# Two transformer blocks on one core: one Strassen pair turned into two plain units, tiles placed in another order, and the loading of x rearranged

## The chip, the core and the metric

The kernel runs on one core of a Trainium2 chip. The metric is device time in microseconds of one execution. Before the change the median of three runs is 2495.06 us (2494.91 to 2496.38).

## The reference, cut to what matters

Two blocks over 1024 tokens with 1024 channels, in float32. Block one is gated linear attention beside a short convolution, then a gated feed-forward network of width 2816. Block two is spatial gating beside windowed attention.

```
h = rmsnorm(x, norm1_g); proj = h @ w_in            # 1024 x (2*256 + 2*512 + 16 + 3*512)
gate_logits = p_a @ w_gate_up + b_gate              # p_a: the 16 columns "COL_A = GATE_RANK"
log_a = log_sigmoid(gate_logits) / 16 ; o = gla_chunked(q, k, v, log_a) ...
x = x + concat([o_gla, o_conv]) @ w_out
h2 = rmsnorm(x, norm2_g)
x = x + (silu(h2 @ w_ffn_gate) * (h2 @ w_ffn_up)) @ w_ffn_down
x = rmsnorm(x, norm_f_g)                            # then block two, the same size again
```

## The kernel before

Everything is kept transposed: channels on the 128 partitions, the 1024 tokens along the row. A *unit* is 128 output channels of one projection: 8 slices of the contraction by 2 halves of 512 tokens. Each operand is split into a rounded part and a rest (`x_hi`, `x_lo`, `w_hi`, `w_lo`), and three products are summed, so that a unit is 48 matmuls of 512 columns (L683 hi by hi, L684, L685) into one half, the *slot*, of the PSUM tile `dense` (two slots of two banks). 197 units run in a fixed order. For each, SyncE loads the weights into `w_raw` (`load`), ScalarE makes `w_hi` (`split`, L1028), GpSimd makes `w_lo` (L584), and VectorE takes the result out of PSUM (`scaled`, L1528). Every engine has its own queue in program order, and semaphores join them: `evac` counts results taken out, `mm_done` finished units, `w_lo` split weights.

The gate and up projections of the feed-forward network are 22 tiles of two units each. The first `DIRECT`/2 tiles are plain units. For the others the two units are computed as one *duo*: one level of a Strassen-Winograd scheme over 2x2 quarters, with 7 products of 12 matmuls instead of 8 (84 instead of 96). The products read sums of quarters of x (`x_sums_split`, three of the seven) or quarters of x itself, and the weights' sums are made on VectorE (`weight_sums`, L1716 to L1723). `times` (L831 to L833) issues one product into one of the PSUM banks B7, B5, B1, B6. `hi_half` (ScalarE, L1180) and `lo_half` (GpSimd, L619) fill one of four half-slots of `w_hi` and `w_lo` for one product; `half(p, i)` says which. Product 5 of a duo adds onto bank B7 and waits for `joined`, that is for VectorE's L1773. The raw weights of the duos alternate between `w_raw` and a second buffer in tiles 12 and 13 of `work`.

The finished tiles m go to DRAM (`store_m`) and are read back behind the duos into tiles 12 and 13 of `work` (`load_m`), split (`m_hi` on ScalarE, L1210, `m_lo` on VectorE, L1728), and feed the down projection, whose first unit is U_DOWN.

At the start SyncE asks for the vectors, the weights of unit 0 (the 16 gate columns padded with zeros to 128), x in eight slices with the weights of unit 1 after the fourth, and so on. Unit 0 takes the slices of x as they come; unit 1 follows it. ScalarE writes x_hi (L1059), VectorE x_lo (L1487), then both make the sums of squares for the norm (L1042, L1499), and the token sums (L705) and the spread of the norm's factor (L713) are put between matmuls of units.

Tiles are placed by `place` one behind the other in each partition: x_hi, x_lo (32 KiB each), w_raw, w_hi, w_lo (8 KiB each), then the small tiles vectors (316 bytes), identity, ones, rstd and others, and behind them residual (32 KiB) and work (80 KiB). Worked out from the sizes, work starts 129,856 bytes behind x_hi, which is 31 x 4096 + 2880. x_sums_split, work_split, m_hi, m_lo and the softmax tiles lie inside work; att_q_split, att_k_hi, att_k_lo and att_v_split inside residual.

## Time and profile before

| | us |
|---|---|
| median of three runs | 2495.06 |
| the profiled execution | 2494.21 |
| its span, first to last instruction | 2492.5 |
| TensorE (PE) busy | 2416.4 (97%) |
| PE weight loads (beside the matmuls) | 1987.4 (80%) |
| VectorE (DVE) busy | 1239.6 (50%) |
| ScalarE (ACT) busy | 804.3 (32%) |
| GpSimd (POOL) busy | 644.1 (26%) |
| mean granted TensorE clock, as a share of full speed | 0.987 |

The page's chain of the work that ended last lies on PE for 93% of the span and on DVE for 4%. A matmul's record is longer than the distance to the next one, since they are pipelined: what counts is the distance from start to start. In the rows below a bracket at the end of a line gives the engine's idle time before it and what ended that.

### The profile page before, as it was taken

What the parts mean: (1) busy time and instruction counts of PE and PEld (TensorE: products, weight loads), DVE (VectorE), ACT (ScalarE), POOL (GpSimd) and SP (SyncE); (2) the same over time, 40 slices, a digit from 0 to 9 for tenths busy, and PEclk for the clock granted to TensorE, in tenths of its full rate; (3) what the DMA queues carried; (4) which work ended last, traced back from release to release, by engine and by line L of the source; (5) the groups of instructions that cost most, each with busy time, mean ns of one, the idle gap of its engine ahead of it and who ended that gap; (6) DMA issues with size and microseconds to landing.
All of it is one profiled execution on the core that took longest, in us unless ns stands there. A gap on an engine that the chain in (4) does not pass through costs nothing.

```text
span 2492.5 us, 29802 instructions
## 1 busy us (share of the span) xinstructions
PE 2416.4 (97%) x11248; PEld 1987.4 (80%) x11248; DVE 1239.6 (50%) x1655; ACT 804.3 (32%) x1173; POOL 644.1 (26%) x332
## 2 busy tenths in 40 slices
PE   8999999899999989999999999999999999999997
PEld 6888788678888878888888888877877877878886
DVE  4444673844444443344321102477777787753534
ACT  4422132333233321134211101255555555541221
POOL 2221122345555522222221122111121121122221
PEclk9999899999999999999999999999999999999998
DMA  3111222132222242212222224332322323344223
GB/s 129 43 43 34 85 79 90 66 138 85 92 78 76 77 152 102 85 60 85 101 93 76 78 99 140 100 98 94 118 91 86 110 84 100 110 152 143 92 95 109
DMA packets 66148, 234.63 MB, mean 94 GB/s; under 512 B 7936, under 2 KB 8080, under 8 KB 66064
## 3 DMA queue, kind: packets, MB, share of 16 engines
q1 hardware_dynamic: 51376, 179.98, 22.1%
q10 hardware_dynamic: 14688, 53.48, 5.3%
q8 instruction: 59, 0.97, 0.2%
q14 instruction: 25, 0.20, 0.0%
HBM read 175.76 MB, written 57.67 MB: 94 GB/s over the span
## 4 chain that ended last, share of the span: by engine, by line
PE 93%; DVE 4%; issue 1%; DMA 1%; ACT 1%; DVEq 0%; SPq 0%; POOL 0%; ACTq 0%
PE dense L683 22%; PE dense L685 22%; PE dense L684 22%; PE dense L831 5%; PE dense L833 5%; PE dense L832 5%; PE aux L956 2%; PE aux L940 2%; PE aux L941 1%; PE aux L969 1%; PE aux L968 1%; PE aux L903 1%; DVE residual L1733 1%; DVE att_p_lo L1924 1%; PE aux L713 0%
## 5 line engine op out<-in xcount | busy, mean ns | idle before, releaser
L683 PE MATMUL dense<-x_hi,w_hi 128*128 128x512 f32 x2000 | 809.4, 405 | 14.2 <-DVE x_lo L1487 13.0
L685 PE MATMUL dense<-x_hi,w_lo 128*128 128x512 f32 x2000 | 783.5, 392 | 0.0
L684 PE MATMUL dense<-x_lo,w_hi 128*128 128x512 f32 x2000 | 782.4, 391 | 0.0
L584 POOL TENSOR_TENSOR w_lo<-w_raw,w_hi 128x1024 fp32r<-128x1024 f32 x157 | 382.5, 2436 | 1414.0 <-ACT w_hi L1028 1405.9
L1028 ACT CAST w_hi<-w_raw 128x1024 fp32r<-128x1024 f32 x156 | 163.9, 1051 | 886.2 <-PE dense L685 863.2
L683 PEld LDWEIGHTS dense<-x_hi,w_hi 128*128 128x128 f32 x2000 | 378.1, 189 | 84.9 <-issue 15.3
L685 PEld LDWEIGHTS dense<-x_hi,w_lo 128*128 128x128 f32 x2000 | 377.0, 188 | 81.5
L684 PEld LDWEIGHTS dense<-x_lo,w_hi 128*128 128x128 f32 x2000 | 378.5, 189 | 67.6 <-issue 1.2
L1528 DVE TENSOR_TENSOR work<-dense,rstd 128x1024 f32<-128x1024 f32 x95 | 116.0, 1221 | 401.1 <-PE dense L685 395.2
L619 POOL TENSOR_TENSOR w_lo<-w_sums,w_hi 128x512 fp32r<-128x512 f32 x80 | 122.2, 1539 | 142.8 <-ACT w_hi L1180 142.8
L683 PE MATMUL dense<-work_split,w_hi 128*128 128x512 f32 x352 | 138.0, 392 | 1.1 <-DVE work L1785 1.1
L1356 ACT CAST att_p_hi<-aux 128x512 fp32r<-128x512 f32 x192 | 92.1, 479 | 144.6 <-PE aux L956 144.2
L685 PE MATMUL dense<-work_split,w_lo 128*128 128x512 f32 x352 | 138.2, 393 | 0.0
L831 PE MATMUL dense<-x_hi,w_hi 128*128 128x512 f32 x320 | 128.3, 401 | 9.7 <-DVE work L1773 9.7
L684 PE MATMUL dense<-work_split,w_hi 128*128 128x512 f32 x352 | 137.1, 390 | 0.0
L1924 DVE TENSOR_TENSOR att_p_lo<-aux,att_p_hi 128x512 fp32r<-128x512 f32 x192 | 106.3, 554 | 59.6 <-ACT att_p_hi L1356 57.3
L833 PE MATMUL dense<-x_hi,w_lo 128*128 128x512 f32 x320 | 127.2, 397 | 0.0
L832 PE MATMUL dense<-x_lo,w_hi 128*128 128x512 f32 x320 | 126.8, 396 | 0.0
L1680 DVE TENSOR_TENSOR residual<-dense,residual 128x1024 f32<-128x1024 f32 x32 | 39.2, 1225 | 158.7 <-PE dense L685 158.7
L831 PE MATMUL dense<-x_sums_split,w_hi 128*128 128x512 f32 x240 | 95.9, 400 | 9.7 <-DVE work L1528 9.7
L1346 ACT ACTIVATE att_p_late<-att_p_late,softmax_stats 128x640 f32<-128x640 f32 (+1 forms) x64 | 63.5, 993 | 102.0 <-DVE softmax_stats L1905 101.9
L833 PE MATMUL dense<-x_sums_split,w_lo 128*128 128x512 f32 x240 | 95.1, 396 | 0.0
(236 smaller groups left out, 3318.1 us busy)
## 6 DMA issues: line engine op xcount, KB each, us to landing
w_raw<-weights SPq DMA_DIRECT2D x177, 512.0 KB, 3.8
kept_qkv<-work ACTq DMA_DIRECT2D x24, 512.0 KB, 2.6
kept_m<-work ACTq DMA_DIRECT2D x22, 512.0 KB, 2.6
work<-kept_m SPq DMA_DIRECT2D x22, 512.0 KB, 3.5
w_raw_b<-weights SPq DMA_DIRECT2D x20, 512.0 KB, 4.3
residual<-xT SPq DMA_DIRECT2D x16, 512.0 KB, 6.6
kept_x<-residual ACTq DMA_DIRECT2D x16, 512.0 KB, 2.7
att_q<-kept_qkv SPq DMA_DIRECT2D x32, 256.0 KB, 4.0
```

The costliest lines, as they stand in the source:

```text
L584: pool.tensor_tensor(WL[:, u.slot], WR[:, u.slot], WH[:, u.slot].bitcast(f32), ALU.subtract).then_inc(w_lo, 1)
L619: pool.tensor_tensor(WL[:, h // 2, at4], quarter(p, i), WH[:, h // 2, at4].bitcast(f32), ALU.subtract).then_inc(*((d_lo, 1) if i < 6 else ...
L683: pe.matmul(dst, WH[:, u.slot, k], hi, start=(k == 0), stop=False)
L684: pe.matmul(dst, WH[:, u.slot, k], lo, start=False, stop=False)
L685: last = pe.matmul(dst, WL[:, u.slot, k], hi, start=False, stop=(k == nk - 1))
L831: pe.matmul(bank(b), wh, hi[:, j], start=(first and j == 0), stop=False, skip_group_check=True)
L832: pe.matmul(bank(b), wh, lo[:, j], start=False, stop=False, skip_group_check=True)
L833: last = pe.matmul(bank(b), wl, hi[:, j], start=False, stop=(j == 3), skip_group_check=True)
L1028: act.copy(WH[:, u.slot], WR[:, u.slot]).then_inc(w_hi, 1)
L1356: act.copy(PH[:, k % 2, lo:HALF], PA[:, bank, lo:HALF]).then_inc(ph, 1)
L1528: return dve.tensor_tensor(dst, PD[:, u.slot], R[:], ALU.mult).then_inc(evac, 1)
L1924: dve.tensor_tensor(PL[:, k % 2, lo:HALF], PA[:, bank, lo:HALF], PH[:, k % 2, lo:HALF].bitcast(f32), ALU.subtract).then_inc(pl, 1)
```

## The change

**The pairs.** `DIRECT` goes from 4 to 6 and `DUOS` from 20 to 19: tile 2 becomes two plain units, and the duos start one tile later, with another parity of buffers (`w_pair`, `m_buffer`). In the first duo the banks change places: products 0 and 1 go to slot 1 (B7, B5 = 2, 3), so that PE waits only for `evac` of the last unit but one. `weight_sums(0)` and the three `lo_sum` move between the plain units on VectorE, and the sum that GpSimd split is now VectorE's (`lo_sum(2)`). `half` skips one half-slot at duos 4, 8 and 12. In the last duo VectorE splits two tiles m ahead of L1773's successor instead of four, and SyncE asks for four of them instead of two ahead of the weights of U_DOWN.

VectorE, from the second plain unit to the first join of duo 0 (L1528/L1575 take a unit out of PSUM; w_sums are the weights' sums, x_lo and x_sums_split the rests that the duo reads; L1773/L1825 is what product 5 waits for). Before:

```order
L1702 TENSOR_TENSOR x_sums_split<-x_sum,x_sums_split 128x2048
L1716 TENSOR_TENSOR w_sums<-w_raw_b 128x512
L1719 TENSOR_TENSOR w_sums<-w_sums,w_raw_b 128x512
L1528 TENSOR_TENSOR work<-dense,rstd 128x1024
L1748 TENSOR_TENSOR x_sum<-residual 128x2048
L1702 TENSOR_TENSOR x_sums_split<-residual,x_sums_split 128x2048
L1752 TENSOR_TENSOR residual<-residual,x_sum 128x4x512
L1528 TENSOR_TENSOR work<-dense,rstd 128x1024
L1707 TENSOR_TENSOR x_lo<-residual,x_hi 128x4x512
L1698 TENSOR_TENSOR work<-work 128x1024
L1707 TENSOR_TENSOR x_lo<-residual,x_hi 128x4x512 x3
L1773 TENSOR_TENSOR work<-p_p_96,dense 128x512
```

and now:

```order
L1795 TENSOR_TENSOR x_sum<-residual 128x2048
L1750 TENSOR_TENSOR x_sums_split<-residual,x_sums_split 128x2048
L1575 TENSOR_TENSOR work<-dense,rstd 128x1024
L1802 TENSOR_TENSOR residual<-residual,x_sum 128x4x512
L1750 TENSOR_TENSOR x_sums_split<-x_sum,x_sums_split 128x2048
L1575 TENSOR_TENSOR work<-dense,rstd 128x1024
L1764 TENSOR_TENSOR w_sums<-w_raw 128x512
L1575 TENSOR_TENSOR work<-dense,rstd 128x1024
L1746 TENSOR_TENSOR work<-work 128x1024
L1755 TENSOR_TENSOR x_lo<-residual,x_hi 128x4x512 x3
L1825 TENSOR_TENSOR work<-p_p_96,dense 128x512
L1755 TENSOR_TENSOR x_lo<-residual,x_hi 128x4x512
```

All sums of x now stand ahead of the last plain unit but one; behind the last unit's L1575 stand one product of gates and three x_lo, and the fourth x_lo has gone behind the join.

VectorE in the last duo (L1728/L1776 with work_split are the splits of tiles m; L1785/L1840 frees the last bank, for which U_DOWN waits). Before:

```order
L1728 TENSOR_TENSOR work_split<-work,work_split 128x1024 x4
L1767 TENSOR_TENSOR p_p_96<-p_p_96,dense 128x512
L1773 TENSOR_TENSOR work<-p_p_96,dense 128x512
L1775 TENSOR_TENSOR work<-work,dense 128x512
L1728 TENSOR_TENSOR work_split<-work,work_split 128x1024
L1785 TENSOR_TENSOR work<-p_p_96,dense 128x512
```

and now:

```order
L1776 TENSOR_TENSOR work_split<-work,work_split 128x1024 x2
L1821 TENSOR_TENSOR p_p_96<-p_p_96,dense 128x512
L1825 TENSOR_TENSOR work<-p_p_96,dense 128x512
L1827 TENSOR_TENSOR work<-work,dense 128x512
L1776 TENSOR_TENSOR work_split<-work,work_split 128x1024 x2
L1840 TENSOR_TENSOR work<-p_p_96,dense 128x512
```

Two of the four splits went from ahead of the join to behind it.

**The start.** SyncE asks for x first; the vectors go through ScalarE's queue. Unit 0 (16 columns) is now computed with a stationary tile of 32 columns: the rounded part of the 16 columns and its rest beside each other, so that two matmuls a slice and half do (32 in all instead of 48). The gate's small weights are loaded twice, onto 32 rows, which adds the two parts. Unit 1 runs together with it, three slices behind. Ahead of both stand ten matmuls over the tile `ones`, which need no load. PE at the start, before:

```order
L683 MATMUL dense<-x_hi,w_hi 128x512
L684 MATMUL dense<-x_lo,w_hi 128x512
L685 MATMUL dense<-x_hi,w_lo 128x512
L683 MATMUL dense<-x_hi,w_hi 128x512
L684 MATMUL dense<-x_lo,w_hi 128x512
```

and now (the fourth slice of the 32 columns and the first of unit 1 among them):

```order
L729 MATMUL aux<-ones 128x128 x10
L739 MATMUL dense<-x_hi,w_hi 32x512
L740 MATMUL dense<-x_lo,w_hi 32x512
...
L739 MATMUL dense<-x_hi,w_hi 32x512
L740 MATMUL dense<-x_lo,w_hi 32x512
L751 MATMUL dense<-x_hi,w_hi 128x512
L752 MATMUL dense<-x_lo,w_hi 128x512
L753 MATMUL dense<-x_hi,w_lo 128x512
```

What ran slice by slice for one unit now runs for two.

**The memory.** work (80 KiB) and residual (32 KiB) are placed right behind x_lo, ahead of w_raw, w_hi, w_lo and the small tiles. work now starts 65,536 bytes behind x_hi, a multiple of 4096, and w_hi 188,416 bytes behind it instead of 73,728.

**Smaller ones.** The token sums of norm 1 are put into unit 2 after its seventh group of three matmuls, the spread after its fourteenth; the spread of norm 2 three groups earlier.

```diff
-U_GU, TILES, DIRECT, DUOS = 33, 22, 4, 20
+U_GU, TILES, DIRECT, DUOS = 33, 22, 6, 19
+T_DUO = DIRECT // 2
+        WK = place("work", [20, S])
+        XR = place("residual", [KT, S])
...
-        B7, B5, B1, B6 = 0, 1, 2, 3
+        B7, B5, B1, B6 = 2, 3, 0, 1
...
         def half(p, i):
-            return (7 * p + i + 2) % 4
+            return (7 * p + i + 2 + min(p // 4, 3)) % 4
...
-            sp.dma_start(VEC[:], vecs).then_inc(vec_in, 16)
-            load(Unit(0))
             for k in range(KT):
                 sp.dma_start(XR[:, k], xT[k]).then_inc(x_in[k], 16)
-                if k == 3:
-                    load(Unit(1))
+                if k < 2:
+                    load(Unit(k))
...
             def load_duo(p):
                 if p == 0:
+                    sp.wait_ge(w_lo, U_DUO)
+                elif p == 1:
                     sp.wait_ge(mm_done, U_OUT + KT)
...
-            load_m(0)
-            load_m(1)
+            for t in range(4):
+                load_m(t)
...
-            unit(Unit(0), ready=(x_ready, 0))
+            for _ in range(WARM):
+                pe.matmul(PA[:, 3, 0:P], ONES[:], ONES[:], start=True, stop=True)
+            for k in range(KT + LAG):
+                if k < KT:
+                    rank_part(k)
+                if k >= LAG:
+                    q_part(k - LAG)
...
             for p in range(DUOS):
-                pe.wait_ge(evac, U_DUO)
                 if p:
                     pe.wait_ge(joined, 4 * p)
                 else:
+                    pe.wait_ge(evac, U_DUO - 1)
                     pe.wait_ge(t_lo, 1)
...
                 if p:
                     pe.wait_ge(p12, p)
                 else:
+                    pe.wait_ge(evac, U_DUO)
                     pe.wait_ge(b_lo, 1)
                 times(p, 2, XHV[:, 0, :, left], XLV[:, 0, :, left], B1, True)
...
+            dve.wait_ge(sp_m[1], 16)
+            scaled(Unit(U_GU + 5), m_buffer(2))
+            gated_tile(2)
             lo_again(0, 0, 0)
-            gated_tile(1)
             lo_again(1, 1, 0)
             lo_again(2, 0, 1)
-            lo_again(3, 1, 1)
```

## Rows read from the trace of the kernel before

**Rows 1.** Waits of PE in the whole span: total us, times, longest us.

```profile
PE dense L683 <- DVE x_lo L1487: 13.0, 4, 9.9
PE dense L831 <- DVE work L1773: 9.7, 2, 6.3
PE dense L831 <- DVE work L1528: 9.7, 1, 9.7
PE dense L683 <- DVE work L1785: 1.1, 1, 1.1
```

**Rows 2.** Timeline of PE at its start: start us, us, instruction.

```profile
10.46 0.63 PE L684 MATMUL dense<-x_lo,w_hi 128*128 128x512 f32 x1
10.89 0.63 PE L685 MATMUL dense<-x_hi,w_lo 128*128 128x512 f32 x1
...
15.52 0.39 PE L684 MATMUL dense<-x_lo,w_hi 128*128 128x512 f32 x1
```

**Rows 3.** Windows behind PE's waits: us, PE busy, granted clock, DMA share, GB/s.

```profile
491.20:507.80 16.60, 16.57 (x60) 0.83 0.26 95
511.20:530.00 18.80, 18.80 (x70) 0.84 0.15 50
886.40:896.00 9.60, 8.64 (x24) 0.67 0.46 144
```

**Rows 4.** Timelines of DVE, ACT, POOL and PE, x arriving and unit 2's weights.

```profile
14.06 6.19 DVE L1487 SCALAR_TENSOR_TENSOR x_lo<-residual,vectors,x_hi 128x1024 fp32r<-128x1024 f32 x4 [0.72 <-ACT x_hi L1059]
16.89 1.15 ACT L1059 ACTIVATE x_hi<-residual,vectors 128x1024 fp32r<-128x1024 f32 x1 [0.29 <-DMA residual<-xT]
29.62 2.81 POOL L584 TENSOR_TENSOR w_lo<-w_raw,w_hi 128x1024 fp32r<-128x1024 f32 x1 [14.04 <-ACT w_hi L1028]
34.36 1.84 PE L705 MATMUL aux<-ones,work 128*128 128x1 f32 x16
```

**Rows 5.** Timeline of DVE around the first duo.

```profile
474.26 0.68 DVE L1716 TENSOR_TENSOR w_sums<-w_raw_b 128x512 f32<-128x512 f32 x1
...
483.56 6.47 DVE L1752 TENSOR_TENSOR residual<-residual,x_sum 128x2048 f32<-128x2048 f32 x1
489.95 1.21 DVE L1528 TENSOR_TENSOR work<-dense,rstd 128x1024 f32<-128x1024 f32 x1
...
494.26 2.33 DVE L1698 TENSOR_TENSOR work<-work 128x1024 f32<-128x1024 f32 x1
...
505.24 4.49 DVE L1707 TENSOR_TENSOR x_lo<-residual,x_hi 128x2048 fp32r<-128x2048 f32 x2 [6.46 <-ACT x_hi L1167]
```

**Rows 6.** Timelines of SyncE and DVE around the last duo.

```profile
875.44 27.87 SPq L451 DMA_DIRECT2D work<-kept_m  x7
...
882.50 2.49 DVE L1728 TENSOR_TENSOR work_split<-work,work_split 128x1024 fp32r<-128x1024 f32 x2 [9.19 <-ACT work_split L1210]
885.69 0.69 DVE L1773 TENSOR_TENSOR work<-p_p,dense 128x512 f32<-128x512 f32 x1
```

**Rows 7.** Timeline of DVE: two of a kind, one unit or one duo apart.

```profile
540.58 1.53 DVE L1789 TENSOR_TENSOR work<-work 128x1024 f32<-128x1024 f32 x1 [0.80 <-ACT work L1195]
559.83 1.53 DVE L1789 TENSOR_TENSOR work<-work 128x1024 f32<-128x1024 f32 x1 [0.80 <-ACT work L1195]
...
1506.84 1.23 DVE L1528 TENSOR_TENSOR work<-dense,rstd 128x1024 f32<-128x1024 f32 x1 [9.65 <-PE dense L685]
1517.71 1.22 DVE L1528 TENSOR_TENSOR work<-dense,rstd 128x1024 f32<-128x1024 f32 x1 [9.65 <-PE dense L685]
...
368.62 1.23 DVE L1680 TENSOR_TENSOR residual<-dense,residual 128x1024 f32<-128x1024 f32 x1 [5.77 <-PE dense L685]
379.60 1.22 DVE L1680 TENSOR_TENSOR residual<-dense,residual 128x1024 f32<-128x1024 f32 x1 [5.23 <-PE dense L685]
```

**Rows 8.** The page's costliest groups: busy us, mean ns, idle before.

```profile
L683 PE MATMUL dense<-x_hi,w_hi 128*128 128x512 f32 x2000 | 809.4, 405 | 14.2 <-DVE x_lo L1487 13.0
L619 POOL TENSOR_TENSOR w_lo<-w_sums,w_hi 128x512 fp32r<-128x512 f32 x80 | 122.2, 1539 | 142.8 <-ACT w_hi L1180 142.8
```

**Rows 9.** Timeline of PE in the windowed attention.

```profile
1847.71 0.40 PE L683 MATMUL dense<-x_hi,w_hi 128*128 128x512 f32 x1
...
1849.33 0.40 PE L685 MATMUL dense<-x_hi,w_lo 128*128 128x512 f32 x1
```

More of the change, by code:

```diff
@@ L206, in two_blocks @@
         XL = place("x_lo", [KT, S], f32r)
+        WK = place("work", [20, S])
+        XR = place("residual", [KT, S])
+        wk, xr = at["work"], at["residual"]
         WR = place("w_raw", [2, KT, P])
@@ L217, in two_blocks @@
         STAT = place("softmax_stats", [4, 4])
-        WGU = place("gate_up_w", 2 * P, rows=RANK)
-        XR = place("residual", [KT, S])
-        WK = place("work", [20, S])
-        wk, xr = at["work"], at["residual"]
+        WGU = place("gate_up_w", 2 * P, rows=2 * RANK)
         TMP = 16
+        WARM, LAG = 10, 3
         MH = place("m_hi", [8, S], f32r, wk)
@@ L348, in half, with held @@
         def half(p, i):
-            return (7 * p + i + 2) % 4
+            return (7 * p + i + 2 + min(p // 4, 3)) % 4
+        def held(p, i):
+            same = [r for r in range(7 * p + i) if half(r // 7, r % 7) == half(p, i)]
+            return (same[-1] // 7, same[-1] % 7) if same else None
         def w_pair(p):
-            return WR if p % 2 else WRB
+            return WRB if p % 2 else WR
         def quarter(p, i):
@@ L469, in _ @@
                              ).then_inc(w_raw[u.slot], 16)
-            for t in range(2, 8):
+            for t in range(4, 8):
                 load_m(t)
@@ L595, in _ @@
             pool.memset(ONES[:], 1.0).then_inc(consts, 1)
-            for u in range(U_OUT + 2):
+            pool.wait_ge(w_hi, 1)
+            pool.tensor_tensor(WH[:, 0, :, RANK:2 * RANK], WR[:, 0, :, 0:RANK], WH[:, 0, :, 0:RANK].bitcast(f32),
+                               ALU.subtract).then_inc(w_lo, 1)
+            for u in range(1, U_OUT + 2):
                 split(Unit(u))
@@ L722, in _, with rank_part, q_part @@
             pe.wait_ge(consts, 1)
-            unit(Unit(0), ready=(x_ready, 0))
+            for _ in range(WARM):
+                pe.matmul(PA[:, 3, 0:P], ONES[:], ONES[:], start=True, stop=True)
+            def rank_part(k):
+                if k == 0:
+                    pe.wait_ge(w_lo, 1)
+                pe.wait_ge(x_ready, k + 1)
+                for t in range(2):
+                    tok = slice(t * HALF, (t + 1) * HALF)
+                    dst = PD[0:2 * RANK, 0, tok]
+                    pe.matmul(dst, WH[:, 0, k, 0:2 * RANK], XH[:, k, tok], start=(k == 0), stop=False)
+                    last = pe.matmul(dst, WH[:, 0, k, 0:2 * RANK], XL[:, k, tok], start=False, stop=(k == KT - 1))
+                if k == KT - 1:
+                    last.then_inc(mm_done, 1)
+            def q_part(k):
+                if k == 0:
+                    pe.wait_ge(w_hi, 2)
+                    pe.wait_ge(w_lo, 2)
+                for t in range(2):
+                    tok = slice(t * HALF, (t + 1) * HALF)
+                    dst = PD[:, 1, tok]
+                    pe.matmul(dst, WH[:, 1, k], XH[:, k, tok], start=(k == 0), stop=False)
+                    pe.matmul(dst, WH[:, 1, k], XL[:, k, tok], start=False, stop=False)
+                    last = pe.matmul(dst, WL[:, 1, k], XH[:, k, tok], start=False, stop=(k == KT - 1))
+                if k == KT - 1:
+                    last.then_inc(mm_done, 1)
+            for k in range(KT + LAG):
[3 more added lines that the diff above has]
+                    q_part(k - LAG)
             def gate_logits():
-                pe.wait_ge(tab_in, 32)
+                pe.wait_ge(tab_in, 48)
                 pe.wait_ge(a_there, 1)
@@ L796, in norm_sums @@
                 last.then_inc(o_ss, 1)
-            norm1 = {1: beside(g15=[lambda: token_sums(8, WK[:, TMP + 2])]),
-                     2: beside(g10=[lambda: spread(1, WK[:, TMP + 3])])}
-            for u in range(1, U_OUT):
+            norm1 = {2: beside(g6=[lambda: token_sums(8, WK[:, TMP + 2])], g13=[lambda: spread(1, WK[:, TMP + 3])])}
+            for u in range(2, U_OUT):
                 unit(Unit(u), between=norm1.get(u))
@@ L1051, in rstd @@
                 act.copy(dst, one(PA[:, bank:bank + 2])).then_inc(rs, 1)
+            act.dma_start(VEC[:], vecs).then_inc(vec_in, 16)
             act.preload_act_table(ACT.Sqrt)
-            split(Unit(0))
             act.wait_ge(vec_in, 16)
@@ L1059, in _ @@
                 act.activation(XH[:, k], XR[:, k], ACT.Copy, scale=vec(V_G1 + k)).then_inc(xh, 1)
-                if k == 3:
-                    split(Unit(1))
+                if k == 0:
+                    act.wait_ge(w_raw[0], 16)
+                    act.copy(WH[:, 0, :, 0:RANK], WR[:, 0, :, 0:RANK]).then_inc(w_hi, 1)
+                if k == 1:
+                    act.wait_ge(w_raw[1], 16)
+                    act.copy(WH[:, 1], WR[:, 1]).then_inc(w_hi, 1)
             for k in range(KT):
@@ L1217, in _ @@
             hi_sum(1, XV[:, 0, :, HALF:S])
+            split(Unit(U_GU + 4))
+            silu_gate(1)
+            hi_sum(2, XSUM[:])
+            split(Unit(U_GU + 5))
+            store_m(1)
             hi_half(0, 0)
             hi_half(0, 1)
-            silu_gate(1)
-            hi_sum(2, XSUM[:])
+            silu_gate(2)
             hi_half(0, 2)
@@ L1778, in _ @@
                 else:
[L1779 removed]
+                    m_lo(2)
+                    m_lo(3)
                 dve.wait_ge(prod, 6 * p + 6)
```

90 lines of the change are left out of this document (46 added, 44 removed).

## The prediction

> **What bounds the kernel now.** I read the page first: PE is busy for 97% of the span and holds 93% of the chain. So only three things can move the time: PE waiting, the number of its matmuls, and the distance from one to the next. Next came PE's waits [rows 1]. The reader is to see that they are few: 9.9 us before the first matmul, 9.7 us on L1528 and up to 6.3 us on L1773 at L831, all three in stretches that the change rewrites (19.4 us in all behind L1528 and L1773). Then the windows behind these waits [rows 3]: PE is busy there at a mean clock of 0.83, 0.84 and 0.67, so after each wait it runs a while at 1.2 instead of 2.4 GHz. The same is seen at the start: the first matmuls stand 0.43 us apart, and at 15.5 us the record shortens from 0.63 to 0.39 us [rows 2]. Last came the distances in undisturbed stretches, taken from VectorE's taking out, which follows PE [rows 7]: 10.87 us for a unit that reads x_hi and x_lo (226.5 ns for each of 48), 10.98 us for one that reads work_split, 19.25 us for a duo (229.2 ns for each of 84).
>
> **The pair made into two units.** 2 x 10.87 - 19.25 = **+2.5 us**, all on PE.
>
> **The first duo.** Today PE stands still for 9.7 us until 491.2 us, so from 481.5: the last plain unit waits in PSUM behind a sum that takes VectorE 6.47 us from 483.56, its L1528 begins at 489.95, and product 0 may not start before it [rows 5]. Later product 5 waits, 3.4 us (9.7 - 6.3, rows 1), because two x_lo from 505.24 to 509.7 stand ahead of the join [rows 5]. Behind the waits (1 - 0.83) x 16.6 = 2.8 and (1 - 0.84) x 18.8 = 3.0 us go to the clock [rows 3]. Together 18.9 us. In the new order I lay VectorE's queue beside PE's, with durations from the same rows. lo_sum(0) ends near 473.5, since the spread is earlier by about 1 us. L1575 for the third unit, the sum and lo_sum(1) end by 479. The fourth unit ends on PE at 481.5, so VectorE now waits for PE, and takes unit, gate, sum and lo_sum(2) until 488.6. The fifth unit ends at 492.4, the weights' sums follow until 497.4, and the sixth ends at 503.3 us, when the first two products have had all they need for some 5 us. They take 5.5 us, and behind them product 2 needs the first x_lo: 1.2 for the unit, 1.2 to 2.3 for the gate, 2.3 for x_lo, 4.7 to 5.8 us. That is a wait of 0 to 0.5 us. The fourth x_lo behind the join delays the weights' sums by 2.3 us, and VectorE's next L1836, which frees bank B7 for duo 1, to about 0.6 us after PE would want it. What queues behind it on VectorE has room in later duos, where it idles. I take 1.0 us for both (bounds 0 and 3.4, the wait that stands there today). So **-17.9 us**. SyncE asks for the first duo's weights only behind w_lo of the last unit, about 486 us; 1 MB is due at 493.7, on a queue that loads nothing else then, which I cost at nothing.
>
> **The last duo.** L1773 at 885.69 comes behind two splits at 882.50, which came behind 9.19 us of waiting for tiles m, asked for at 875.44 behind 1 MB of weights [rows 6]. In the new order the two splits stand behind the join, and the tiles are asked for earlier. Saved: 6.3 us of waiting and (1 - 0.67) x 9.6 = 3.2 us of clock [rows 1, 3]. Late next is the split m_lo(4) ahead of L1840: its tile is loaded only when m_lo(2) is done, so U_DOWN starts some 1.7 us behind the last product instead of 1.1 [rows 1]; m_lo(6) and m_lo(7) come within 1 to 4 us of their turn. I take +0.6 (bounds 0 and 3). **-8.9 us**.
>
> **half().** Skipping a half-slot in three duos makes three halves each wait for the product three back instead of four. Two products last 5.5 us; GpSimd's 1.54 [rows 8] and a shorter cast of ScalarE fit. Nothing; bounds 0 and 3 x 1.5 = 4.6.
>
> **The start.** The last slice of x comes at 16.8, ScalarE is through at 18.04, but VectorE only at 20.25, and GpSimd's w_lo for unit 2 ends at 32.43, 12.2 later, held by the squares on ScalarE. Unit 1 with its token sums ends at 36.2 us [rows 4]. The same ten transfers of 512 KB stand ahead of the last slice as before, so it comes at most 0.5 us sooner, and x_lo is complete near 19.2. Adding the 12.2, unit 2 can begin at 31.4. PE has 80 matmuls instead of 96 by then; begun at about 7.5 us, with 0.43 us spacing until some 15.4 to 19 us and 0.227 behind, and held by x until 12.5, they end at 30 to 32. 36.2 - 31.4 less the 1.8 us of L705, which move into unit 2: **-3.0 us** (bounds -5 and, with the slow spacing to the end, +7).
>
> The sum so far is +2.5 - 17.9 - 8.9 - 3.0 = -27.3 us.
>
> **The memory.** Units of one shape differ by what they read: 10.98 against 10.87 us, and the duo's 84 matmuls take 19.25 instead of 84 x 226.5 ns = 19.02 us [rows 7]. Neither more instructions nor a wait goes with it. What differs is the place: x_hi and x_lo start at one multiple of 4096 bytes plus a constant, as the weights do; work, which holds x_sums_split, work_split and m_hi, starts 2880 bytes off it and further up. After the change work is both nearer and on the multiple. Whether offset or distance is the cause, or something that stays, no row tells. If it goes: 19 x 0.23 = 4.4 for the duos and 24 x 0.11 + 8 x 0.08 = 3.3 for the 32 units fed from work (eight of them have 36 matmuls), 7.7 us. In the attention, whose tiles lie in residual and work, seven spacings from 1847.71 to 1849.33 give 231.4 ns [rows 9]; 2304 matmuls (32 units of 48 and 768 of scores and outputs) at 4.9 ns less are another 11.3 us. Bounds below: w_hi and w_lo move far up, and if that costs the x_hi matmuls the 2.3 ns that work costs today, 6960 of them are +16.0 us. I take **-7.7**: both causes that I can name lead to it, while the attention's tiles mix with x_hi's and lie partly in residual, now higher up.
>
> The Trainium skill says of SBUF (SBUF — State Buffer, "SBUF: two separate sides") that only the port pair shared by GpSimd and VectorE makes engines contend, and that PE's own ports never wait on anyone. By that rule the place would be free and this term 0. The rows do show a difference between units, which it doesn't explain.
>
> 2494.21 - 27.3 - 7.7 = 2459.2 for the profiled execution; the median stood 0.85 above it, so 2460.
>
> **The rivals.**
> - The memory changes nothing: 2468. For it: nothing shows that the place is the cause. Against it: the same two values return with the same tiles in distant stretches.
> - The attention gains too: 2449.
> - The weights' new place costs 2.3 ns on each x_hi matmul, and nothing is gained: 2468 + 16 = 2484.
> - New waits at the first duo. If GpSimd holds VectorE on each of the three x_lo as it did at 494.26 (2.33 instead of 1.2 us, rows 5), product 2 and duo 1 wait some 2 us each and the clock falls once or twice: +8, so 2468. That lock is what the Trainium skill states on the same page and section: VectorE with two SBUF inputs and GpSimd exclude each other. The trace agrees, by that 2.33 us.
> - The start runs at 1.2 GHz to the end. Ten short matmuls at 1 us are followed by idleness until x is there, as at 481.5, where the clock fell. The 32-column matmuls and the waits for x between them may not bring it up: 80 x 0.427 + 7.5 = 41.6 instead of 31.4, +10: 2470.
> - Slower: the weights' new place costs what the attention pays today, 4.9 ns, on all 9120 dense matmuls of 512 columns (3 x (2000 + 352 + 320 + 240 + 128)): +44.7 - 27.3 = +17.4, 2512. It decides from 27.3 / 9120 = 3.0 ns on. Against it: the largest step seen between units of one shape is 2.3 ns.
>
> **How the numbers follow.** Chances: the forecast 0.28, memory neutral 0.24, attention too 0.18, weights dearer 0.08, new waits 0.08, slow start 0.10, slower 0.04. The range 2446 to 2478 takes in all but the two dear places of the weights. 0.2% is 5 us, about what a measurement of this kernel tells from no change; only the last case reaches it: faster 0.95, same 0.02, slower 0.03.
>
> **What would show it.** The wait of L831's successor on L1528 gone and those on L1825 under 1 us; the granted clock 1.00 from the sixth plain unit to U_DOWN; unit 2's first matmul near 31.4 us, and w_lo rather than PE the last to come; L1844 18 times 19.0 us apart instead of 19.25, and the L1728 of the output projection 10.87 apart. If the duos still stand 19.25 apart, the memory term was wrong. If units that read x_hi stand over 10.87 apart, the place of the weights matters, and each 0.1 us more costs about 14 us over the 145 units' worth of such matmuls. The whole is wrong if PE still stands still for microseconds at either end of the duos.

## The result and the profile after

The changed kernel takes **2461.77 us** (median of 4 runs, 2458.66 to 2463.76), the kernel before 2494.98 us beside it (4 runs, 2487.03 to 2496.38). The ratio is 0.9872, 95% interval 0.9848 to 0.9896: 33 us, or 1.3%, faster. The forecast was 2460, with a range of 2446 to 2478. The profiled execution took 2463.76 us, with a span of 2462.0, so 30.5 us less than the profiled one of before.

From the page of the changed kernel (the last two rows: busy us, mean ns, idle before):

```profile
PE 2405.7 (98%) x11264; PEld 1982.9 (81%) x11264; DVE 1238.4 (50%) x1649; ACT 800.9 (33%) x1166; POOL 635.7 (26%) x326
PE 95%; DVE 3%; issue 1%; DMA 1%; ACT 0%; DVEq 0%; SPq 0%
L688 PE MATMUL dense<-x_hi,w_hi 128*128 128x512 f32 x2000 | 807.6, 404 | 4.5 <-DVE x_lo L1534 3.1
L868 PE MATMUL dense<-x_sums_split,w_hi 128*128 128x512 f32 x228 | 88.8, 390 | 1.2 <-DVE work L1836 1.2
```

The bound is what it was: PE is busy for 98% of the span and holds 95% of the chain. L688 has the same 2000 matmuls as L683 had [rows 8], with hardly a wait before them. What became of PE's waits [rows 1] (total us, times, longest):

```profile
PE aux L979 <- DVE softmax_stats L1961: 25.8, 16, 1.9
PE aux L832 <- ACT work L1168: 3.3, 1, 3.3
PE dense L688 <- DVE x_lo L1534: 3.1, 3, 1.3
...
PE dense L688 <- DVE work L1840: 1.6, 1, 1.6
...
PE dense L868 <- DVE work L1836: 1.2, 1, 1.2
```

The 9.7 us behind L1528 and the 9.7 behind L1773 are gone. In their place stand 1.2 us between the first duo and the second (L1836 frees the bank that the second one needs) and 1.6 at U_DOWN (1.1 before). Both stay without a fall of the clock, as the windows show (us, then the busy times of five engines, PE first, then the granted clock, the DMA share and GB/s); the third is the place of the 3.3 us wait of L832, where the clock did fall:

```profile
480.00:530.00 50.00, 48.80 (x214) 39.46 (x213) 33.95 (x24) 18.46 (x23) 26.69 (x15) 1.00 0.29 100
862.00:876.00 14.00, 12.39 (x55) 9.92 (x55) 8.00 (x7) 5.24 (x6) 2.40 (x1) 1.00 0.65 228
262.00:276.00 14.00, 13.43 (x36) 9.42 (x37) 4.88 (x5) 2.69 (x4) 4.07 (x2) 0.53 0.13 37
```

VectorE around the first duo, the counterpart of [rows 5] (start us, us, instruction, idle before):

```profile
484.38 2.28 DVE L1750 TENSOR_TENSOR x_sums_split<-x_sum,x_sums_split 128x2048 fp32r<-128x2048 f32 x1
488.54 1.22 DVE L1575 TENSOR_TENSOR work<-dense,rstd 128x1024 f32<-128x1024 f32 x1 [1.89 <-PE dense L690]
...
499.42 1.23 DVE L1575 TENSOR_TENSOR work<-dense,rstd 128x1024 f32<-128x1024 f32 x1 [6.02 <-PE dense L690]
500.68 1.76 DVE L1746 TENSOR_TENSOR work<-work 128x1024 f32<-128x1024 f32 x1
502.36 8.88 DVE L1755 TENSOR_TENSOR x_lo<-residual,x_hi 128x2048 fp32r<-128x2048 f32 x3
```

VectorE now waits for PE ahead of both last units (1.89 and 6.02 us), where PE had waited for it. The three x_lo take 8.88 us, 2.28, 3.38 and 3.38, instead of the 2.25 each of [rows 5]. GpSimd splits weights at the same time, and its three halves take 3.4, 3.3 and 3.3 us, where one that meets none of these x_lo takes 1.3:

```profile
502.38 3.41 POOL L628 TENSOR_TENSOR w_lo<-w_sums,w_hi 128x512 fp32r<-128x512 f32 x1 [1.02 <-ACT w_hi L1222]
```

The x_lo of 502.36 starts 0.02 us ahead of this half and keeps its 2.28 us, and the half is late by 2.1; each later one of either engine is late by about the rest of what the other had begun. It is the "new waits" rival's mechanism, and its price here is 1.2 us, once, instead of 8.

VectorE's queue is not all that changed here. Before, VectorE stood idle for 6.46 us ahead of its two last x_lo, until ScalarE had written their x_hi [rows 5], and ScalarE wrote both only behind three weight halves that wait for PE's products. The change also puts these two x_hi one and two halves earlier on ScalarE, which the description of the change leaves out. First before, then after:

```profile
503.30 3.71 ACT L1167 CAST x_hi<-residual 128x2048 fp32r<-128x2048 f32 x2
```

```profile
504.53 1.91 ACT L1210 CAST x_hi<-residual 128x2048 fp32r<-128x2048 f32 x1
```

The first of the pair is written 12.1 us behind the start of PE's first product before (491.2) and 5.4 us behind it after (499.15), and the third x_lo follows without idleness.

VectorE around the last duo, the counterpart of [rows 6], and when PE goes on:

```profile
848.43 2.61 DVE L1776 TENSOR_TENSOR work_split<-work,work_split 128x1024 fp32r<-128x1024 f32 x2 [1.25 <-ACT work_split L1252]
...
857.11 2.35 DVE L1776 TENSOR_TENSOR work_split<-work,work_split 128x1024 fp32r<-128x1024 f32 x2
...
862.64 1.23 DVE L1776 TENSOR_TENSOR work_split<-work,work_split 128x1024 fp32r<-128x1024 f32 x1 [1.52 <-ACT work_split L1252]
863.78 0.68 DVE L1840 TENSOR_TENSOR work<-p_p,dense 128x512 f32<-128x512 f32 x1
```

```profile
864.72 0.47 PE L688 MATMUL dense<-work_split,w_hi 128*128 128x512 f32 x1 [1.61 <-DVE work L1840]
```

As forecast, m_lo(4) at 862.64 stands late ahead of L1840, because its tile came late (ScalarE's half of the split waited 2.31 us for the DMA).

The distances of [rows 7], one duo (L1844) and one unit fed from work (L1728) apart:

```profile
541.02 1.52 DVE L1844 TENSOR_TENSOR work<-work 128x1024 f32<-128x1024 f32 x1 [0.80 <-ACT work L1237]
560.06 1.52 DVE L1844 TENSOR_TENSOR work<-work 128x1024 f32<-128x1024 f32 x1 [0.80 <-ACT work L1237]
...
365.23 1.23 DVE L1728 TENSOR_TENSOR residual<-dense,residual 128x1024 f32<-128x1024 f32 x1 [5.67 <-PE dense L690]
376.11 1.23 DVE L1728 TENSOR_TENSOR residual<-dense,residual 128x1024 f32<-128x1024 f32 x1 [5.13 <-PE dense L690]
```

19.04 instead of 19.25 us, and 10.88 instead of 10.98: all units of one shape now take the same time, 226.7 ns a matmul.

Where the 30.5 us came from, read off VectorE's taking out of the same unit in both profiled executions:

| taken out | before | after | gained so far |
|---|---|---|---|
| first unit of the output projection | 357.63 | 354.35 | 3.3 |
| its eighth | 434.54 | 430.51 | 4.0 |
| first unit behind the duos | 907.5 | 875.99 | 31.5 |
| last unit of block one | 1137.3 | 1104.4 | 32.9 |
| end of the span | 2492.5 | 2462.0 | 30.5 |

Nearly all of it lies between the eighth unit and the first behind the duos, with 27.5 us. Behind block one 2.4 us are given back.

### The profile page after: what moved, and what is told of

Read it like the earlier page. It is cut to its first block, busy times and chain, and to the rows that moved or that the text cites. A ratio compares the mean times of both kernels' runs of the same rounds, so it can differ in the third digit from the quotient of the medians.

```text
span 2462.0 us, 29790 instructions
## 1 busy us (share of the span) xinstructions
PE 2405.7 (98%) x11264; PEld 1982.9 (81%) x11264; DVE 1238.4 (50%) x1649; ACT 800.9 (33%) x1166; POOL 635.7 (26%) x326
## 4 chain that ended last, share of the span: by engine, by line
PE 95%; DVE 3%; issue 1%; DMA 1%; ACT 0%; DVEq 0%; SPq 0%
PE dense L688 23%; PE dense L689 23%; PE dense L690 23%; PE dense L870 5%; PE dense L868 5%; PE dense L869 5%; PE aux L995 2%; PE aux L979 2%; PE aux L980 1%; PE aux L1008 1%; PE aux L1007 1%; PE aux L942 1%; DVE att_p_lo L1980 1%; PE aux L718 0%; PE aux L823 0%
## 5 line engine op out<-in xcount | busy, mean ns | idle before, releaser
L688 PE MATMUL dense<-x_hi,w_hi 128*128 128x512 f32 x2000 | 807.6, 404 | 4.5 <-DVE x_lo L1534 3.1
L690 PE MATMUL dense<-x_hi,w_lo 128*128 128x512 f32 x2000 | 782.4, 391 | 0.0
L688 PEld LDWEIGHTS dense<-x_hi,w_hi 128*128 128x128 f32 x2000 | 377.7, 189 | 75.4 <-issue 5.8
L1575 DVE TENSOR_TENSOR work<-dense,rstd 128x1024 f32<-128x1024 f32 x97 | 118.5, 1221 | 406.2 <-PE dense L690 398.7
L688 PE MATMUL dense<-work_split,w_hi 128*128 128x512 f32 x352 | 137.0, 389 | 1.6 <-DVE work L1840 1.6
L868 PE MATMUL dense<-x_hi,w_hi 128*128 128x512 f32 x304 | 118.4, 390 | 0.0
L870 PE MATMUL dense<-x_hi,w_lo 128*128 128x512 f32 x304 | 118.3, 389 | 0.0
L1728 DVE TENSOR_TENSOR residual<-dense,residual 128x1024 f32<-128x1024 f32 x32 | 39.2, 1225 | 155.9 <-PE dense L690 155.9
L979 PE MATMUL aux<-att_k_hi,att_q_split 128*128 128x512 f32 (+1 forms) x192 | 66.5, 346 | 25.8 <-DVE softmax_stats L1961 25.8
L868 PE MATMUL dense<-x_sums_split,w_hi 128*128 128x512 f32 x228 | 88.8, 390 | 1.2 <-DVE work L1836 1.2
```

The costliest lines, as they stand in the source:

```text
L688: pe.matmul(dst, WH[:, u.slot, k], hi, start=(k == 0), stop=False)
L690: last = pe.matmul(dst, WL[:, u.slot, k], hi, start=False, stop=(k == nk - 1))
L868: pe.matmul(bank(b), wh, hi[:, j], start=(first and j == 0), stop=False, skip_group_check=True)
L870: last = pe.matmul(bank(b), wl, hi[:, j], start=False, stop=(j == 3), skip_group_check=True)
L979: pe.matmul(dst, QS[:, i * P:(i + 1) * P], KH[:, c:c + w], start=True, stop=False)
L1575: return dve.tensor_tensor(dst, PD[:, u.slot], R[:], ALU.mult).then_inc(evac, 1)
```

## The experiments

Ratios are against the kernel before, run beside each. Runs with one execution have no ratio and are read by their traces.

**The memory alone, on the kernel before.**

```diff
         XL = place("x_lo", [KT, S], f32r)
+        WK = place("work", [20, S])
+        XR = place("residual", [KT, S])
...
-        XR = place("residual", [KT, S])
-        WK = place("work", [20, S])
```

> The kernel before, with work and residual placed right behind x_lo, ahead of the weights, and nothing else changed. If the place of the tiles is the cause of the shorter distances (19.05 instead of 19.25 us a duo, 10.88 instead of 10.98 a unit that reads work_split), this alone gives them: -7.7 us by the prediction's sum, and about 1.1 ns a matmul in the attention as the changed kernel's trace has it, 2.5 us more: 2485. If the shorter distances come from the new order of the instructions: no change, 2495.

Measured: 2482.64 us (7 runs) against 2492.41, ratio 0.996 [0.9948, 0.9971], so 9.8 us (7.2 to 13). The instructions and their order are those of before; the spacing goes to 226.7 ns in every group fed from work:

```profile
537.38 1.51 DVE L1789 TENSOR_TENSOR work<-work 128x1024 f32<-128x1024 f32 x1 [0.80 <-ACT work L1195]
556.42 1.52 DVE L1789 TENSOR_TENSOR work<-work 128x1024 f32<-128x1024 f32 x1 [0.80 <-ACT work L1195]
```

19.04 us as in the changed kernel. That the place of a tile costs time is shown here by itself.

**Everything but the memory.** The changed kernel with residual and work behind the small tiles, as before.

```diff
-        WK = place("work", [20, S])
-        XR = place("residual", [KT, S])
...
         WGU = place("gate_up_w", 2 * P, rows=2 * RANK)
+        XR = place("residual", [KT, S])
+        WK = place("work", [20, S])
```

> The changed kernel with the tiles placed as before (residual and work behind the small tiles); all else of the change stays. Theory (place): duos 19.25 us again, units of work_split 10.98, and 2462 + 9 = 2471, so 24 us faster than before. Rival (order of the instructions): 2462.

Measured: 2464.9 us (4 runs) against 2492.41, ratio 0.9892 [0.9874, 0.991]. The distances are those of before:

```profile
359.88 1.23 DVE L1728 TENSOR_TENSOR residual<-dense,residual 128x1024 f32<-128x1024 f32 x1 [5.76 <-PE dense L690]
370.87 1.23 DVE L1728 TENSOR_TENSOR residual<-dense,residual 128x1024 f32<-128x1024 f32 x1 [5.25 <-PE dense L690]
```

10.99 us. The time came 6 us below the 2471 that was expected. So the rest brings 27.5 us (22.4 to 31.4) and the memory 9.8, in sum more than the 33 of the whole. The surplus of 4 us is within the intervals. In the profiled executions the clock accounts for it: behind the 3.3 us wait of L832 it stood at 0.91 over the same 14 us, where it stood at 0.53 in the changed kernel:

```profile
262.00:276.00 14.00, 14.00 (x60) 10.16 (x60) 3.83 (x4) 1.64 (x3) 4.07 (x2) 0.91 0.11 37
```

From the eighth unit of the output projection to the first behind the duos this kernel gains 23.7 us, where the changed one gains 27.5. The difference, 3.8 us, is what the memory is worth in the duos.

**Offset or distance? The order of the tiles changed in two ways.** First work and residual behind the three weight tiles, so that work lies 90,112 bytes behind x_hi and *behind* the weights, all on multiples of 4096:

```diff
-        WK = place("work", [20, S])
-        XR = place("residual", [KT, S])
         WR = place("w_raw", [2, KT, P])
         WH = place("w_hi", [2, KT, P], f32r)
         WL = place("w_lo", [2, KT, P], f32r)
+        WK = place("work", [20, S])
+        XR = place("residual", [KT, S])
```

> The changed kernel with work and residual behind w_lo, ahead of the small tiles: work starts 90,112 bytes behind x_hi, a multiple of 4096, and the weights stay where they were before. Theory (the rest over 4096): duos 19.05 us, as in the changed kernel. Rival (distance from the weights or from the start): x_sums_split now reaches from 106 to 155 KB, so that duos lie between 19.05 and 19.25 or at 19.25.

Measured in one run: 2456.47 us. Every spacing is 226.7 ns, so distance plays no part. The run is one of the two fastest single ones of all (2456.36 is the other, with the tiles as in the changed kernel), but the placement need not be the reason: the 3.3 us wait of L832 happened to cost no clock at all (1.00 over 262 to 276 us, against 0.53), which is worth 14 x 0.47 = 6.6 us:

```profile
262.00:276.00 14.00, 14.00 (x65) 10.88 (x66) 4.15 (x5) 1.96 (x3) 4.08 (x2) 1.00 0.12 37
```

Then the small tiles ahead of work and the weights, so that x_hi keeps its place and all else is shifted by the same odd amount:

```diff
         XL = place("x_lo", [KT, S], f32r)
-        WK = place("work", [20, S])
...
         VEC = place("vectors", VECS)
...
         WGU = place("gate_up_w", 2 * P, rows=2 * RANK)
+        WK = place("work", [20, S])
+        XR = place("residual", [KT, S])
+        WR = place("w_raw", [2, KT, P])
+        WH = place("w_hi", [2, KT, P], f32r)
+        WL = place("w_lo", [2, KT, P], f32r)
```

> The changed kernel with the small tiles ahead of work: work 2880 bytes past a multiple of 4096 behind x_hi, but near (72,512 bytes), and the weights 2880 past it too. If what counts is the rest of the moving tile alone: duos partly 229 ns (their x_sums_split products), x_hi units 226.5. If it is the rest of the moving tile against that of the stationary one: x_hi units become dearer (10.98 us) and units of work_split cheap (10.87). If it is distance: all cheap.

Measured in one run: 2496.79 us, 35 us more than the changed kernel. Now the units fed from x_hi are slow and those fed from work are fast (L1575 follows a unit of x_hi, L1728 one of work):

```profile
1454.81 1.23 DVE L1575 TENSOR_TENSOR work<-dense,rstd 128x1024 f32<-128x1024 f32 x1 [9.97 <-PE dense L690]
1466.01 1.23 DVE L1575 TENSOR_TENSOR work<-dense,rstd 128x1024 f32<-128x1024 f32 x1 [9.97 <-PE dense L690]
```

```profile
359.73 1.22 DVE L1728 TENSOR_TENSOR residual<-dense,residual 128x1024 f32<-128x1024 f32 x1 [3.98 <-PE dense L690]
370.61 1.23 DVE L1728 TENSOR_TENSOR residual<-dense,residual 128x1024 f32<-128x1024 f32 x1 [5.67 <-PE dense L690]
```

11.20 us, 233.3 ns a matmul, against 10.88. This is the key run: work is as odd as it was before the change, and fast, because the weights are odd by the same amount. What counts is the difference between the address of the moving tile and that of the stationary one. It is like the "slower" rival of the prediction, but with 6.6 ns on the matmuls that read x_hi or x_lo. On all 6,912 of them that would be 46 us, and 35 arrive. In the attention, where 1,536 of them are, the mean distance grows by 2.4 ns only; that accounts for about half of the difference, and what makes the rest was not looked for.

**Which differences are bad? Gaps of 64, 512, 1024 and 256 bytes** between the weights and work, in the placement of the run before last:

```diff
         WL = place("w_lo", [2, KT, P], f32r)
+        place("gap", 16)
         WK = place("work", [20, S])
```

(`128`, `256` and `64` instead of `16` in the other three; the unit is 4 bytes.)

> As the run with work behind the weights, with 64 bytes left free ahead of work: work starts 64 past a multiple of 4096 behind x_hi and the weights. Theory (any rest against the stationary tile over 4096 counts): units that read work_split above 10.88 us, by up to the 0.1 to 0.3 us seen at rests of 2880 and 1216; x_hi units 10.88. Rival (the rest counts over a smaller power of two, of which 64 is a multiple): all 10.88.

> The same with 512 bytes left free, one slice of a stationary tile. If the rest counts over 512 or less: units that read work_split 10.88 us, duos 19.05. If it counts over more, 10.9 to 11.2 and over 19.1.

> The same with 1024 bytes left free, half a row of the moving operand. If the rest counts over 1024 or less: units that read work_split 10.88 us. If it counts over 2048 or 4096: 10.9 to 11.2.

> As the runs with 64, 512 and 1024 bytes left free ahead of work, with 256. So far rests of 0, 512 and 1024 between moving and stationary tile give 226.7 ns, 64 and 2880 give 229.0, and -2880 gives 233.4. If the rest counts over 256 (2880 and 64 are then both 64, -2880 is 192): units that read work_split 10.88 us, duos 19.05. If it counts over 512 (2880 is then 320): 10.9 to 11.2.

Measured, one run each: 2464.92, 2460.26, 2463.29 and 2463.44 us. The totals say little, since the clock falls differ; the distances say it. Two units fed from work with the gap of 64, then with that of 256:

```profile
364.70 1.23 DVE L1729 TENSOR_TENSOR residual<-dense,residual 128x1024 f32<-128x1024 f32 x1 [5.77 <-PE dense L691]
375.69 1.23 DVE L1729 TENSOR_TENSOR residual<-dense,residual 128x1024 f32<-128x1024 f32 x1 [5.23 <-PE dense L691]
```

```profile
355.25 1.23 DVE L1729 TENSOR_TENSOR residual<-dense,residual 128x1024 f32<-128x1024 f32 x1 [3.94 <-PE dense L691]
366.13 1.23 DVE L1729 TENSOR_TENSOR residual<-dense,residual 128x1024 f32<-128x1024 f32 x1 [5.67 <-PE dense L691]
```

| kernel | moving less stationary address, rest modulo 256 | ns a matmul |
|---|---|---|
| before, work against the weights | 64 (2880 = 11 x 256 + 64) | 228.9 |
| gap of 64 | 64 | 228.9 |
| gaps of 256, 512, 1024 | 0 | 226.7 |
| after, work or x_hi against the weights | 0 | 226.7 |
| small tiles first, x_hi against the weights | 192 (-2880) | 233.3 |
| small tiles first, work against the weights | 0 | 226.7 |

A gap of 64 bytes brings back not only the 10.99 us but the pattern of before within the three products of a group (about 232, 226 and 229 ns). The rest modulo 256 sorts all cases. A rest of 128 was not tried, nor finer steps, and 64 was seen only with work as the moving tile, 192 only with x_hi and x_lo; that the rest alone makes the difference between 228.9 and 233.3 is therefore not shown.

**The identity on a multiple of 256**, by exchanging it with the vectors in the changed kernel, for the attention's short matmuls:

```diff
-        VEC = place("vectors", VECS)
         IDN = place("identity", P)
+        VEC = place("vectors", VECS)
```

> The changed kernel with identity ahead of vectors, so that identity, the operand of the transposes, starts at a multiple of 4096 behind x_hi as all large tiles do, instead of 320 bytes past it. Theory: the 230.3 ns between dense matmuls that remain in the attention come from the change between this rest and the other at each transpose; they fall toward 226.7, on some 1536 matmuls, so 3 to 6 us off: 2457. Rival (they come from the mixture of short and long matmuls): 2462 and 230.3 stays.

Measured: 2462.32 us (4 runs) against 2491.8, ratio 0.9878 [0.9859, 0.9897]: nothing gained. Over 1650 to 2150 us the mean distance from the start of a 512-column matmul to the next start, worked out from all that the trace has at full clock and without a wait, is 231.4 ns before, 230.3 in the changed kernel and 230.3 here. At the very place of [rows 9] the changed kernel has 227.1 ns (1.59 us for seven):

```profile
1817.74 0.40 PE L688 MATMUL dense<-x_hi,w_hi 128*128 128x512 f32 x1
...
1819.33 0.39 PE L690 MATMUL dense<-x_hi,w_lo 128*128 128x512 f32 x1
```

So those seven were a poor sample for 2304 matmuls: most of the 4.9 ns over the plain units' spacing remains. Shorter matmuls stand between the long ones there; that they are the cause was only seen side by side, not tested.

**Twenty matmuls over ones instead of ten.**

```diff
-        WARM, LAG = 10, 3
+        WARM, LAG = 20, 3
```

> The changed kernel with 20 matmuls over ones ahead instead of 10, so that they reach to about 8 us, when the first slice of x is ready. Theory (the gap from 5.7 to 8.0 us let the clock fall back at 9 us): the clock stays at 2.4 GHz, the joint unit ends near 30.4 us instead of 32.6, and unit 2 begins at about 31.5, held by its w_lo: 1.1 us off, within what three rounds can tell, but to be seen in the trace. Rival (waits for x and the 32-column matmuls let it fall anyway): half clock until 19 us again, 32.6.

Measured: 2462.41 us (4 runs) against 2489.9, ratio 0.989 [0.9874, 0.9907]. In the changed kernel PE idles for 2.35 us between the ones and the first slice, and over 9 to 19 us its clock is 0.50; with twenty there is no idle time there, and the clock over the same stretch is 0.83. So it still fell once, from 14.0 to 17.4 us, where it was expected to stay. First the changed kernel, then this one:

```profile
8.02 0.42 PE L739 MATMUL dense<-x_hi,w_hi 128*32 128x512 f32 x1 [2.35 <-POOL w_hi L603]
...
32.60 0.39 PE L688 MATMUL dense<-x_hi,w_hi 128*128 128x512 f32 x1
```

```profile
8.47 0.48 PE L739 MATMUL dense<-x_hi,w_hi 128*32 128x512 f32 x1
...
31.72 0.47 PE L688 MATMUL dense<-x_hi,w_hi 128*128 128x512 f32 x1
```

And GpSimd in this one:

```profile
28.81 2.80 POOL L590 TENSOR_TENSOR w_lo<-w_raw,w_hi 128x1024 fp32r<-128x1024 f32 x1 [16.43 <-ACT w_hi L1067]
```

Unit 2 begins 0.9 us earlier, and then w_lo, done at 31.61, is the last to come. The gain in the trace is near the 1.1 us that was worked out, and too small for the median to tell.

**The banks of the first duo as before**, with VectorE's new order kept.

```diff
-        B7, B5, B1, B6 = 2, 3, 0, 1
+        B7, B5, B1, B6 = 0, 1, 2, 3
...
-                    pe.wait_ge(evac, U_DUO - 1)
+                    pe.wait_ge(evac, U_DUO)
```

> The changed kernel with the banks of the duos as before (B7, B5, B1, B6 = 0, 1, 2, 3), so that the first product waits until the last plain unit is taken out. Theory: PE waits 1.3 us there (a taking out of 1.2), too short for the clock to fall, and less or nothing at product 2: +1 to +1.5 us, 2463. Rival (the banks were what removed the 9.7 us): a wait of several us.

Measured: 2460.76 us (2 runs, 2456.36 and 2465.16, the latter profiled) against 2489.9, ratio 0.9881 [0.9855, 0.9908]. PE's waits from 440 to 530 us:

```profile
PE dense L868 <- DVE work L1575: 1.4, 1, 1.4
PE dense L868 <- DVE work L1836: 0.5, 1, 0.5
```

1.9 us of waiting instead of 1.2, and the clock at 1.00 over 485 to 510 us. At the first duo the exchange of banks is worth 0.7 us. Nearly the whole term of the first duo comes from the rest of the change there: VectorE's sums ahead of the last units, ScalarE's two x_hi earlier, and the third plain tile that makes room for them. No run takes these apart.

Over all the duos this profiled execution gains 23.0 us on the one before instead of 27.5. Of the 4.5 us less, some 4 are lost at U_DOWN:

```profile
PE dense L688 <- DVE work L1840: 2.7, 1, 2.7
```

Measured from PE's last product, the tile for m_lo(4) came 1.1 us later than in the changed kernel, PE waited 2.7 us instead of 1.6, and the clock fell behind it (0.81 over 862 to 880 us). Nothing that depends on the banks shows in that delay. It shows how near the new last duo stands to a fall of the clock.

**The last duo as before**, with four splits ahead of the join and two tiles m asked for early.

```diff
-            for t in range(4):
-                load_m(t)
+            load_m(0)
+            load_m(1)
...
                 if p == DUOS - 1:
-                    m_lo(0)
-                    m_lo(1)
+                    for r in range(4):
+                        m_lo(r)
...
                 else:
-                    m_lo(2)
-                    m_lo(3)
+                    m_lo(4)
```

> The changed kernel with the last duo as before: four tiles m split ahead of the join, two of them asked for ahead of U_DOWN's weights instead of four. Theory: PE waits 6.3 us in product 5, and the clock falls behind it, 3.2 us more, less 0.6 at U_DOWN's start: +8.9 us, 2471. Rival (the tiles come early enough now for another reason): under 2 us.

Measured: 2469.21 us (4 runs) against 2489.9, ratio 0.9921 [0.9904, 0.9938]; the kernels run beside it with the new last duo stand at 2462.41 and 2460.76. The wait is back (PE's waits from 840 to 890 us), and so is the clock's fall behind it:

```profile
PE dense L868 <- DVE work L1825: 6.2, 1, 6.2
PE dense L688 <- DVE work L1839: 1.1, 1, 1.1
```

```profile
858.00:868.00 10.00, 7.36 (x24) 5.63 (x24) 6.11 (x8) 3.13 (x4) 2.36 (x1) 0.71 0.54 162
```

Over the duos this kernel gains 19.9 us on the one before, the changed one 27.5: the last duo is worth 7.6 us. In the medians it is 6.8 and 8.5.

## Why the prediction was right, point by point

| term | forecast | measured in the profiled executions |
|---|---|---|
| pair into two units, first and last duo | -24.3 | -23.7 (everything but the memory, duos) |
| of these, the last duo | -8.9 | -7.6 |
| start | -3.0 | -1.8 |
| memory in the duos | -4.4 | -3.8 |
| memory in the 32 units fed from work | -3.3 | about -3.0 |
| attention | 0 in the sum | -2.5 of spacing, +2.0 of waiting |
| half(), weights' place, SyncE | 0 | nothing seen |

*The bound and the waits.* Right: the removed waits (19.4 us) and the time at half clock behind them (9.0), less 1.7 of new waiting and the 2.5 that the pair costs, are 24.2 of the 30.5 us, and what came instead (1.2 and 1.6 us) was forecast as 1.0 and 1.7. VectorE took the last three units out at 477.66, 488.54 and 499.42 us; forecast were 481.5, 492.4 and 503.3, which is the same to 0.2 us once the 4.0 us gained before are taken off. What VectorE did between them took longer than laid out: the last sum of x ended at 486.66 instead of 484.6, and the three x_lo took 2.96 us in the mean instead of 2.3. Both fell into room that the new order had left. One reading was incomplete: the 3.4 us wait of product 5 before was put down to two x_lo ahead of the join, but VectorE had stood idle for 6.46 us ahead of these, for ScalarE's x_hi. The -23.7 less the last duo's -7.6 leaves -16.1 for the first duo and the pair, against -15.4 forecast.

*The last duo.* Its waits came out within 0.1 us. The term is 1.3 us smaller in the trace mainly because the kernel with the old last duo ran at half clock only from 860.3 to 863.8 us behind its wait, a loss of 1.7 us, where [rows 3] has 3.2.

*The start.* The step "w_lo rather than PE the last to come" failed in the changed kernel's profiled execution. Unit 2's first matmul stands at 32.60 us, forecast 31.4; w_lo ended at 31.48. PE was last, as it ran at half clock until 19.1 us and then at 0.231 us for as long as 32-column matmuls stood between the others. With the same start, unit 2 began at 31.3 to 32.8 us in the other profiled kernels, by where the clock stood at half. In "everything but the memory", with a clock of 0.86 over 9 to 19 us, w_lo was the last:

```profile
31.52 0.47 PE L688 MATMUL dense<-x_hi,w_hi 128*128 128x512 f32 x1 [1.20 <-POOL w_lo L590]
```

So that step is right or wrong by the clock of the execution. Against the 36.06 of before, less the 1.7 of the token sums, -1.8 us remain. The table above shows 3.3 us at this point, because the profiled execution of before also had a fall of the clock near 63 us (0.83 over 60 to 70 us) that the changed one lacked (1.00). Of 3.3 us, 1.7 are that luck. The rival of the slow start didn't come: half clock ended at 19.1.

*The memory.* The mechanism was forecast as the likeliest of several, with the cause (offset or distance) left open; the runs settle it. The Trainium skill's sentence (SBUF — State Buffer, "SBUF: two separate sides") that PE never waits on anyone does not speak of two operands of PE itself. This case's rows differ by 2.2 and 6.6 ns a matmul with the difference of the two tiles' addresses, and by that sentence alone the term would have been 0 and the median some 2468. The sizes were right: by the spacings 20 duos x 0.21, some 3.0 for the units fed from work and 2304 x 1.1 ns in the attention make 9.7 us, and the edit alone measured 9.8. The attention's share was the part that the forecast left to a rival, which had it at 11.3 from too few matmuls.

*Given back.* Behind block one 2.4 us are lost against the one before, although the attention's spacing gains 2.5: the attention's scores wait 25.8 instead of 23.8 us for the softmax, and the clock falls near 1115, 1671 and 2122 us in the changed kernel but only near 1852 in the one before, at 1.7 us each. These falls differ between the profiled kernels, and the changed kernel's own runs spread over 5 us. No term of the forecast stood for them.

*How near, and by what luck.* The profiled execution was forecast at 2459.2 and took 2463.76 us, 4.6 more; the median came within 2 us of its 2460. The larger misses have both signs: 1.2 us at the start, 1.3 at the last duo and 5.4 of waits and clock falls behind block one on one side, 2.5 of the attention's spacing and 1.7 of the clock near 63 us on the other. That the median met the forecast so closely is in part luck; that it lies some 33 us below is not.

## What to carry to other kernels

Lay the waiting engine's queue beside the engine that it waits for, with durations from the trace, before moving anything, and look at what that queue waits for in its turn: the new order on VectorE and ScalarE was worth some 15 us, the cost of the added plain pair taken off, the banks 0.7. Behind each wait of several microseconds look for time at half clock, since here it added half again to what the waits cost (9.0 to 19.4 us). And place the tiles that TensorE reads in fp32 so that the distance from moving to stationary tile is a multiple of 256 bytes: one odd-sized tile ahead of the others cost 10 us here, and in an unlucky order 35.

## What the runs showed of the hardware

- The start-to-start time of fp32 matmuls with 512 columns and a new stationary tile each is 226.7 ns at full clock when the address of the moving tile less that of the stationary one is a multiple of 256 bytes; 228.9 with a rest of 64 (a gap of 64 bytes alone does it), 233.3 with a rest of 192. Neither distance nor which lies first matters (226.7 in both orders).
- In the duos, products fed from x_hi were slower before the change too (228.8 against 226.7 ns after), though x_hi and the weights had a rest of 0. The loss stands only in the twelve matmuls right behind a product that read x_sums_split, the tile with the rest of 64: 230.8 ns in the mean over 560 to 830 us, and 226.7 in the products from x_hi that follow. Three starts of the kernel before, twelve matmuls apart, show it (2.77 us, then 2.72):

```profile
569.12 0.40 PE L831 MATMUL dense<-x_hi,w_hi 128*128 128x512 f32 x1
...
571.89 0.39 PE L831 MATMUL dense<-x_hi,w_hi 128*128 128x512 f32 x1
...
574.61 0.39 PE L831 MATMUL dense<-x_hi,w_hi 128*128 128x512 f32 x1
```

  So in the duos the change from one rest to another costs time too. It is the same with the gap of 64 bytes and gone where both rests are 0; why is open.
- Ten matmuls of 128 columns over ones (20 records, 4.60 us) did bring the clock up: the first slice, at 8.02 us, has records of 0.39 us. But the 2.35 us of idleness between were followed by half clock from 9 to 19 us. With the same ten, five of the other ten profiled kernels ran the first slice at half clock already, four as the changed one, and in one the clock fell within it (first record 0.41 us, third 0.63).
- A wait of 3.0 to 3.3 us near 262 us, which all kernels have, was followed by a clock of 0.53 over 14 us in the changed kernel, 0.91 in another and 1.00 in a third. Waits of 1.2 and 1.6 us at the duos left it at 1.00, one of 2.7 us did not. Of the changed kernel's seven waits of 1.9 us in the attention two were followed by a fall of 3.4 us. Two falls of that length stand behind no wait at all but behind matmuls that use little of the array, while PE counts as busy: near 1115 us in the changed kernel behind 32 of one column (L710, 3.69 us), near 63 us in the one before behind 8 whose stationary tile has 16 rows (L731, 3.81 us). One such wait makes up to 7 us of difference between single runs, more than most edits here are worth.
- While GpSimd split weights, VectorE's x_lo, with both inputs in SBUF, took 3.38 us instead of 2.28, and GpSimd's halves 3.3 to 3.4 us instead of 1.3. The one that began second was late by about what the first had left to do: they took turns.
